# Seven half-size products a pair in the delta-net's projections, and products without a reader behind the norms' sums

## The reference

```python
proj = h @ w_in                      # q, k, v, z for 8 heads of 128, and a, b
qkv = silu(causal_dwconv(qkv, conv_w))          # 4 taps along the sequence
q = l2norm(q) * dk ** -0.5;  k = l2norm(k)
kk = where(strict, (k * beta) @ k.T * decay, 0)
sol = triangular_solve(kk + eye, [v * beta, k * beta * exp(gc)])
... per block: v_new = u - w @ state; o = q exp(g) @ state + qk @ v_new; state = ...
o = o * rsqrt(mean(o * o) + 1e-6) * norm_w * silu(z)
y = o @ w_out
```

```python
y = (x - mean(x)) * rsqrt(var(x) + eps) * g + b
```

## Time and profile before

| | |
|---|---|
| time, median of 3 runs | 2706.67 us (2705.37 to 2707.93) |
| time of the profiled execution | 2705.38 us |
| its span | 2703.6 us, granted clock 0.994 in the mean |
| TensorE busy | 2611.0 us |
| VectorE, ScalarE, GpSimd busy | 1650.5, 682.9, 146.1 us |
| delta-net, heads 0 to 7 | about 86 to 520 us of the span, 55.4 us a head |

### The profile page before, as it was taken

One profiled execution on the slowest core, in us unless ns is written; L12 is line 12 of the kernel. 1 busy time (PEld: TensorE's weight loads), 2 busy tenths in 40 slices (PEclk: granted clock), 3 DMA queues, 4 the chain that ended last, 5 costly groups with the idle time before them and its releaser, 6 DMA issues.

```text
span 2703.6 us, 30522 instructions
## 1 busy us (share of the span) xinstructions
PE 2611.0 (97%) x11992; PEld 1963.3 (73%) x11992; DVE 1650.5 (61%) x2935; ACT 682.9 (25%) x1293; POOL 146.1 (5%) x114
## 2 busy tenths in 40 slices
PE   7999999999999999999999999998999998999999
PEld 2566666568888877888887888885445454888888
DVE  2666667487776454554647877654465486766652
ACT  2334343131111021112102111003443364222200
POOL 0000010010000020000001000001121000000000
PEclk9999999999999999999999999999999999999999
DMA  8121122135443321121122544331021310122121
GB/s 351 63 94 63 63 75 91 54 125 187 159 154 146 117 98 70 67 98 67 63 80 81 190 155 180 143 122 67 31 80 63 125 63 32 63 94 94 60 91 53
DMA packets 25357, 275.02 MB, mean 102 GB/s; under 512 B 3576, under 2 KB 4472, under 8 KB 8192
## 3 DMA queue, kind: packets, MB, share of 16 engines
q1 hardware_dynamic: 21760, 268.39, 26.6%
q10 hardware_dynamic: 3456, 4.69, 0.5%
HBM read 270.97 MB, written 2.10 MB: 101 GB/s over the span
## 4 chain that ended last, share of the span: by engine, by line
PE 90%; DVE 5%; ACT 2%; DMA 1%; issue 1%; POOL 0%; SPq 0%; DVEq 0%; ACTq 0%; POOLq 0%
PE bank L537 29%; PE bank L619 14%; PE bank L2150 10%; PE bank L1264 8%; PE bank L2551 4%; PE bank L412 4%; PE bank L1937 4%; PE bank L1396 2%; PE bank L1414 2%; PE bank L2235 1%; DMA arena<-w_ada 1%; PE bank L2544 1%; PE bank L2999 1%; PE bank L1422 1%; PE bank L2683 1%
## 5 line engine op out<-in xcount | busy, mean ns | idle before, releaser
L537 PE MATMUL bank<-HT,ring 128*128 128x256 f32 x1056 | 252.4, 386 | 9.8 <-ACT HT L945 7.4
L1264 PE MATMUL bank<-HT,ring 128*128 128x512 f32 x512 | 250.3, 597 | 5.6 <-ACT arena L1550 5.6
L537 PE MATMUL bank<-arena,ring 128*128 128x256 f32 x1056 | 249.5, 379 | 0.0
L537 PE MATMUL bank<-arena 128*128 128x256 f32 x1056 | 249.5, 379 | 0.0
L537 PEld LDWEIGHTS bank<-HT,ring 128*128 128x128 f32 x1056 | 202.5, 193 | 45.2 <-issue 15.5
L537 PEld LDWEIGHTS bank<-arena,ring 128*128 128x128 f32 x1056 | 200.6, 190 | 27.3
L537 PEld LDWEIGHTS bank<-arena 128*128 128x128 f32 x1056 | 200.6, 190 | 27.3
L619 PE MATMUL bank<-arena,ring 128*128 128x256 f32 x936 | 207.3, 380 | 9.4 <-ACT arena L691 5.6
L619 PEld LDWEIGHTS bank<-arena,ring 128*128 128x128 f32 x936 | 177.0, 190 | 37.0 <-ACT arena L691 6.8
L1185 ACT ACTIVATE arena<-bank,ffc 128x512 f32<-128x512 f32 x66 | 51.3, 778 | 486.7 <-DVE bank L1093 486.7
L2551 PE MATMUL bank<-HT,ring 128*128 128x512 f32 x320 | 148.2, 604 | 3.0 <-ACT HT L985 3.0
(11 more groups left out here) (470 smaller groups left out, 4216.7 us busy)
## 6 DMA issues: line engine op xcount, KB each, us to landing
ring<-w_ada SPq DMA_DIRECT2D x33, 2048.0 KB, 8.2
ring<-w_up SPq DMA_DIRECT2D x33, 2048.0 KB, 7.6
ring<-w_down SPq DMA_DIRECT2D x24, 1408.0 KB, 6.1
ring<-w_gdn SPq DMA_DIRECT2D x7, 2048.0 KB, 8.7
ring<-w_ret_qk SPq DMA_DIRECT2D x4, 2048.0 KB, 7.7
ring<-w_ret_v SPq DMA_DIRECT2D x4, 2048.0 KB, 7.6
ring<-w_ret_g SPq DMA_DIRECT2D x4, 2048.0 KB, 7.7
ring<-w_ret_out SPq DMA_DIRECT2D x4, 2048.0 KB, 7.6
```

What stands on the lines that cost most here:

```text
L537: last = nc.tensor.matmul(out_, w[:, k, :], x[:, k, :], start=(first and k == 0), stop=(k == 3), skip_group_check=not first)
L1264: last = nc.tensor.matmul(B[u % 2][:, :], w[:, u, k, :], HT[:, k, :], start=(k == 0), stop=(k == KC - 1))
```

## The change

**Projections.** The four units of a head become two pairs, (q, k) and (z, v), and a pair is computed by seven products of half the size where eight would be plain. The weights of a pair are the quarters A11, A12 (first unit, channels 0 to 3 and 4 to 7) and A21, A22; the inputs are cut at channel chunk 4 and at token 256. Four combinations of the inputs (`gdn_T`) are made once on VectorE. Four combinations of the weights are made for each pair on GpSimd, in place in the ring (S3 = A11 - A21, S2 = A22 - S3, S1 = A11 + S2, S4 = A12 - S2). The products M1 to M7 are four steps each of 128 x 128 by 128 x 256, 28 steps a pair, 56 a head. ScalarE keeps M1 and M7 (`m1`, `m7`) and the first result (`c11`); VectorE adds up the others (`t`, `U2`, `c21`, `c22`, `c12`), into SBUF for q, k and v and into the bank for z. The first tap moves to ScalarE (`tap`), the other three stay on VectorE and read the sums from SBUF (`dve_taps`).

**Order.** A head's tail now has 14 steps of the head after next, each level 7 of the next: three ahead of TE, two behind TE and two behind DT. The taps of v move into the head's own levels 1 and 2, vtok from level 2 to 3, gcb from 3 to 4, `normed` from 2 to 5; khat moves behind the inverse of level 6. `zs` is doubled, and the gate is made in the tail before the scan. Table `sel` is no longer loaded; a column of `ident`, broadcast, takes its place (`head_row`).

**Products without a reader.** `pe_keep_clock(n)` multiplies `ident` by itself n times into bank 6, where nothing reads it. It stands behind `pe_sums` of the delta-net's output (13), of the feed-forward networks 0 (13) and 1 (24), of retention (13) and of the mixed output (9), and behind `pe_squares` (11).

```diff
@@ pe_gdn_out, pe_mix_out, pe_down, pe_ret_out and the tensor block @@
             pe_sums(pe, tag, OUT_ORDER[-1], True)
+            pe_keep_clock(pe, 13)
...
+        def pe_keep_clock(pe, n):
+            for _ in range(n):
+                nc.tensor.matmul(B[6][:, 0:P], ident[:, :], ident[:, :], start=True, stop=True)
...
+            if has_mean:
+                pe_keep_clock(pe, 13 if i == 0 else 24)
@@ the projections @@
-                last = nc.tensor.matmul(B[u % 2][:, :], w[:, u, k, :], HT[:, k, :], start=(k == 0), stop=(k == KC - 1))
+        GDN_UNITS = ((0, 1), (3, 2))
+        GDN_ORDER = ("M1", "M7", "M2", "M4", "M5", "M6", "M3")
+        GDN_AHEAD = (0, 2, 4, 6, 8, 10, 12, 13, 14)
+        def pe_steps(pe, h, s0, s1):
+            for s in range(s0, s1):
+                p, name, k = s // PAIR, GDN_ORDER[s % PAIR // 4], s % 4
...
+                elif name == "M7":
+                    out_, w, x, first = Bx[:, 0:TH], A21, gdn_T[2], True
+                    if k == 0:
...
+                        if p:
+                            pe.wait_ge(dve_done, at("dve", "gdn", "c12", h, 0))
+                        elif h:
+                            pe.wait_ge(act_done, at("act", "gdn", "z", h - 1))
+                        pe.wait_ge(pool_done, at("pool", "gdn", "S3", h, p))
...
+                last = nc.tensor.matmul(out_, w[:, k, :], x[:, k, :], start=(first and k == 0), stop=(k == 3), skip_group_check=not first)
@@ the fills @@
+                        s = GDN_AHEAD[-1] + 7 * (l - 1)
+                        pe_steps(pe, h + 1, s + (0, 3, 5, 7)[n0], s + (0, 3, 5, 7)[n1])
@@ ScalarE @@
             def gate(h):
-                act.wait_ge(pe_done, at("pe", "gdn", "proj", h, 3))
-                if h:
-                    act.wait_ge(dve_done, at("dve", "gdn", "gated", h - 1))
-                nc.scalar.activation(G["zs"], B[1][:, :], ACT.Silu).then_inc(act_done, AC.tick("gdn", "z", h))
+                act.wait_ge(dve_done, at("dve", "gdn", "c12", h, 1))
+                if h >= 2:
+                    act.wait_ge(dve_done, at("dve", "gdn", "gated", h - 2))
+                nc.scalar.activation(zs[h % 2], B[1][:, :], ACT.Silu).then_inc(act_done, AC.tick("gdn", "z", h))
@@ VectorE, one head @@
                     if more:
-                        if l < 5:
-                            dve_conv4(dve, h + 1, (l - 1) // 2, 2 * ((l - 1) % 2), 2 * ((l - 1) % 2) + 1)
-                        elif l == 5:
-                            dve_conv4(dve, h + 1, 2, 0, 1)
-                        else:
-                            dve_conv4(dve, h + 1, 2, 3, 4)
-                            khat(h + 1)
+                        if l == 1:
+                            dve_taps(dve, h, 2, 1, 2)
+                        elif l == 2:
+                            ta[1]()
+                            dve_taps(dve, h, 2, 3, 4)
+                        elif l == 3:
+                            ta[4]()
+                        elif l == 4:
+                            dve_taps(dve, h + 1, 1, 3, 4)
+                        elif l == 5:
+                            dve_taps(dve, h + 1, 0, 3, 4)
+                        else:
+                            tb[0]()
                         inverse()
...
+                        if l == 1:
+                            dve_taps(dve, h, 2, 2, 3)
+                            ta[0]()
+                        elif l == 2:
+                            ta[2]()
+                            ta[3]()
+                        elif l == 3:
+                            dve_taps(dve, h + 1, 1, 1, 3)
+                        elif l == 4:
+                            dve_taps(dve, h + 1, 0, 1, 3)
...
+                        elif l == 6:
+                            tb[1]()
+                            tb[2]()
+                            khat(h + 1)
+                            tb[3]()
+                            tb[4]()
                             qhat(h + 1)
@@ GpSimd @@
+            def others(h, p):
+                A11, A12, A21, A22 = gdn_quarters(h, p)
+                pool.wait_ge(pe_done, at("pe", "gdn", "M7", h, p))
+                pool.wait_ge(pool_done, at("pool", "gdn", "S3", h, p))
+                nc.gpsimd.tensor_tensor(A21, A22, A21, ALU.subtract).then_inc(pool_done, PO.tick("gdn", "S2", h, p))
+                pool.wait_ge(pool_done, at("pool", "gdn", "S2", h, p))
+                pool.wait_ge(pe_done, at("pe", "gdn", "M1", h, p))
+                nc.gpsimd.tensor_tensor(A11, A11, A21, ALU.add).then_inc(pool_done, PO.tick("gdn", "S1", h, p))
+                pool.wait_ge(pe_done, at("pe", "gdn", "M2", h, p))
+                nc.gpsimd.tensor_tensor(A12, A12, A21, ALU.subtract).then_inc(pool_done, PO.tick("gdn", "S4", h, p))
...
+            for h in range(GH - 1):
+                third(h + 1, 1)
+                if h + 2 < GH:
+                    third(h + 2, 0)
+                others(h + 1, 1)
+                decay(h + 1)
+                if h + 2 < GH:
+                    others(h + 2, 0)
+                query(h + 1)
```

More of the change, by code:

```diff
@@ new lines, in program @@
+        assert o <= 19968
+        raw_q = region(19968, T)
+        raw_k = wab[:, :, :].rearrange("p k n -> p (k n)")
+        raw_v = sel[:, 0:4, :].rearrange("p i c -> p (i c)")
+        gdn_raw = (raw_q, raw_k, raw_v)
+        zs = [G["zs"], sel[:, 4:8, :].rearrange("p i c -> p (i c)")]
+        gdn_T = [region(21504 + 1024 * n, 4, TH) for n in range(4)]
+        gdn_m1, gdn_m7, gdn_t, gdn_U2 = (HT[:, n, TH:T] for n in range(4))
+        GDN_UNITS = ((0, 1), (3, 2))
+        GDN_ORDER = ("M1", "M7", "M2", "M4", "M5", "M6", "M3")
@@ L1399, in pe_gdn @@
                         osum(h - 1)
-                    if l == 2:
+                    if l == 3:
                         vtok(h)
-                    if l == 3 and more:
+                    if l == 4 and more:
                         gcb(h + 1)
-                    fill(4 * l - 4, 4 * l - 2)
+                    fill(l, 0, 1)
                     pe.wait_ge(dve_done, at("dve", "gdn", "Tm", h, l))
@@ L1569, in act_gdn @@
                 load(name, dst, late_in)
-            for u in range(2):
-                silu(0, u)
-                square(0, u)
+            tap(0, 1)
+            tap(0, 0)
+            keep_m1(0, 1)
+            keep_m7(0, 1)
+            silu(0, 1)
+            square(0, 1)
             raw(0)
-            silu(0, 2)
+            silu(0, 0)
+            square(0, 0)
             gate(0)
             roots(0)
+            keep_m1(1, 0)
             decays(0)
+            tap(0, 2)
+            keep_m7(1, 0)
+            keep_c11(1)
             lower(0)
@@ L1582, in act_gdn @@
                     oroot(h - 1)
+                silu(h, 2)
+                if more:
+                    tap(h + 1, 1)
                 act.wait_ge(pe_done, at("pe", "gdn", "vtok", h))
@@ L1589, in act_gdn @@
                 if more:
-                    silu(h + 1, 0)
-                    square(h + 1, 0)
+                    tap(h + 1, 0)
+                    keep_m1(h + 1, 1)
+                    keep_m7(h + 1, 1)
                     raw(h + 1)
@@ L1601, in act_gdn @@
                 if more:
-                    silu(h + 1, 2)
+                    gate(h + 1)
+                    if h + 2 < GH:
+                        keep_m1(h + 2, 0)
+                    tap(h + 1, 2)
+                    if h + 2 < GH:
+                        keep_m7(h + 2, 0)
+                        keep_c11(h + 2)
                     lower(h + 1)
@@ L1783, in dve_gdn @@
                         inverse()
-                        if l == 2 and h:
+                        if l == 1:
+                            dve_taps(dve, h, 2, 1, 4)
+                        if l == 2:
                             normed(h - 1)
@@ L3251, in _ @@
             pe_squares(pe, "norm4")
+            pe_keep_clock(pe, 11)
             pe_hg(pe)
@@ L3302, in _ @@
                         if u == 0:
-                            table("sel", sel[0:GH], gdn_in)
                             table("ones", ones, gdn_in)
@@ L3461, in layout @@
     A["xT"] = x["x"][0].reshape(T, KC, P).transpose(2, 1, 0)
-    for k in ("ident", "maskL", "maskU", "causal", "ones", "sel", "comb", "headsum", "rot", "cmask", "ret_cos", "ret_sin", "ret_D"):
+    for k in ("ident", "maskL", "maskU", "causal", "ones", "comb", "headsum", "rot", "cmask", "ret_cos", "ret_sin", "ret_D"):
         A[k] = t[k]
```

240 lines of the change are left out of this document (174 added, 66 removed).

## The result

The changed kernel takes 2715.6 us (median of 15 runs, 2707.6 to 2719.8) where the kernel before took 2706.7 in 15 runs beside it: the ratio is 1.0029, 95% interval 1.0021 to 1.0036. The forecast was 2688, 0.7% faster. The profiled execution has a span of 2714.5 us, 10.9 more than before.

The account below looks back on a forecast made before the run. TensorE, busy for 97% of the span, was taken as the bound. Delta-net -12.3 and products without a reader -6.4 bring the span from 2703.6 to 2684.9 us, the median from 2706.67 to 2688.0; range 2668 to 2704.

Parts of the forecast that it names:

- end of the tail: Delta-net tail, before the next head's TE: VectorE's chain up to Tm becomes the limit, TensorE standing 2.2 us for Tm.
- wait for z: Tail of the kernel before: TensorE stands 1.8 us for the gate z, a wait that the change removes.
- S3 of the head after next: GpSimd operation in the delta-net's levels: comes when its load lands, near level 2, against VectorE's PSUM readers.
- Levels, 33.2: Levels 1 to 6 of a delta-net head: 34.8 us falls to 32.7, plus 0.5 of delays beside GpSimd, 33.2.
- Tail, 20.4: From TE's end in level 6 to the next head's first TE: 20.4 us against 20.6, bounded by VectorE.
- Entry, +0.5: Start of the delta-net: fewer product costs, but T sums, S3 and longer queues; +0.5 us, with 2.5 either way.
- Heads 6 and 7, and head 0: Head 6 saves only the levels' 1.6 us; head 7 keeps its products; six heads with a pair ahead save 11.2.
- Delta-net, -12.3: Whole delta-net: six heads -11.2, head 6 -1.6, entry +0.5, together -12.3 us.
- Products, -6.4: Products without a reader keep the clock behind norms 0, 1, 2 and 5: 1.6 us each; nothing behind 3 and 4.
- (e): Rival: eight GpSimd operations hold VectorE's chain for their whole length, 10.2 us a head: 2740, mild form 2715; chance 0.13.
- (b): Rival: GpSimd's work falls in gaps of VectorE, TensorE stays the bound, six heads at -4.5: 2671 us; chance 0.15.

Follow-up runs that it names:

- bridge: The changed kernel with nine more products without a reader ahead of TE of level 1 in heads 1 to 6: 2707.9 us (1.0002).
- narrow: The changed kernel with S1 to S4 on GpSimd cut to 8 of their 512 elements a partition, waits and order kept: 2686.6 us (0.9918).
- reordered kernel: The changed kernel with GpSimd's order changed: S2 and S1 stay in the tail; S4, S3 and qe wait for levels' E subtractions: 2685.2 us (0.9920).
- second run: The changed kernel with the products without a reader left out, so the projections alone: 2720.9 us (1.0042).
- sixth run: The kernel with GpSimd's operations reordered, plus XT's eight multiplications by ALPHA moved from the entry into level 5 of the heads: 2684.5 us (0.9913).

## Why the prediction was wrong

The step that failed is the end of the tail: "So the tail stays at 20.4 against 20.6: VectorE takes the place of z, and TensorE stands 2.2 us for Tm." The wait is there and has its size. It was priced as a wait for a wait, and that was wrong twice. The wait for z was read as 1.8 us, but TensorE was idle for 0.94 us of that, so the idle time rose from 0.94 to 2.12. And behind the longer one TensorE's clock fell in six tails of six. The levels behind stand 3.12 + 3.13 + 1.5 + 1.57 + 3.14 + 1.49 = 14.0 us above the 33.1 of head 0, of which the falls are 9.0, by the bridge. I had worked out what a fall costs behind the norms, from the earlier trace rows, and did not ask the same question of a wait that I was myself lengthening. That these falls need the long wait is shown by the bridge (no wait, no fall) and by the narrow and the reordered S operations (waits of 0.9 us and none, no fall). The weight load that runs beside the first slow stretch (DMA share 0.94) is not their cause either: the reordered kernel has it in the same place (0.97 from 143.2 us on) with the clock at 1.00. That the wait always brings one is not so: head 0 here and head 4 of the second run have it without a fall.

The other 5.0 us belong to a second sentence of the prediction: "S3 of the head after next comes when its load lands, near level 2, against PSUM readers." It meets the ada step of level 2, whose inputs are both in SBUF, and costs a microsecond a head where TensorE is on time: in heads 1 to 5 of the bridge and in head 4 of the second run.

The other terms, against the span of the profiled execution:

- **Levels, 33.2.** Head 0: 33.10, right. Reordered, with the collision of level 2 gone as well: 33.02.
- **Tail, 20.4.** 20.75; the five GpSimd operations of the tail, followed one by one, were right within 0.4 us. This gives 6 x 0.35 = 2 us of the miss.
- **Entry, +0.5 "with two GpSimd lengths (2.5) either way".** It is +5.1, outside its own bounds. VectorE's chain there is longer than I counted: XT's eight multiplications take 5.98 us where they took 2.77, and the last T sum and D and E 1.6 to 2.3 each. The reordered kernel takes back 1.7, with E at its own length. The rest was moved but not removed by the sixth run; what it would take to shorten the entry stays open, ScalarE's queue being next.
- **Heads 6 and 7, and head 0.** I credited head 0 with the saving of the others, though its levels were 34.0 before and not 34.8 (0.7); head 7 and the last tail grew by 0.4 and 0.1.
- **Delta-net, -12.3.** It is +9.6 (the last TE of level 6 starts at 515.3 us instead of 505.7). The difference of 21.9 is 14.0 + 2.1 + 4.6 + 0.7 + 0.5, in the order of the levels of heads 1 to 6, the tails, the entry, head 0, and head 7 with the last tail.
- **Products, -6.4.** Behind norm 0 they give 1.1, norm 2 1.1 to 1.2, norm 5 1.7, and 0.3 behind norms 3 and 4 together; behind norm 1 nothing, since VectorE makes the sums of the next stage late in its turn. That is 4.3 of 6.4. Against it three slow stretches that the kernel before had not, at 1731.9, 1909.4 and 2185.9 us, cost 1.8, 2.5 and 1.4. The middle one stands at a wait for GpSimd that is 1.05 us in the kernel before and 3.58 here: TensorE comes there earlier, by what the products behind norm 3 gave, and waits it away. With the products alone that wait is 3.56 us, with a fall; with the projections alone 1.95, with a fall too. Of the other two, each at a wait as long as in the kernel before, the runs do not show the cause.

Of the rivals, (e) ends on the side where the measurement came out, at 2715 in its mild form. The mechanism that it names is about half of the delta-net's miss: S operations held VectorE's chain for 0.35 us a tail above my count, for a microsecond in level 2 of five heads (hidden here, open in the bridge), and in the entry, but not for their whole length. The clock did the rest, 9.0 of the 21.9 us. Rival (b), TensorE as the bound with 50.9 us a head, is what the reordered kernel shows: 33.02 + 18.48 = 51.5.

## What to carry to other kernels

- When a change puts a wait of some 2 us in front of TensorE, price the wait and the time behind it: here the falls behind six waits of 2.1 us cost another 9 us, where the reordered kernel, without waits or falls in the tails, is worth 22.6 (2707.8 less 2685.2).
- Read a wait from the engine's idle time, not from the chain: the chain's 1.8 us for z held 0.9 us of work.
- Work moved to GpSimd is placed by what VectorE does meanwhile. The same operations in the changed kernel's order cost some 30 us more than in the reordered one: in the two traces 13.6 us in the six tails, 14.4 in the levels of heads 1 to 6 (falls 9.0 by the bridge, the rest mostly the collision in level 2), and 3.4 in the entry and elsewhere. Waits that delay GpSimd were the whole repair.
- Before products are added to keep the clock, look at which waits come next: where falls were taken away others appeared, and the net was 2 to 3.5 us for six places.

## What the hardware did that I had not expected

- The clock fell behind waits of 2.1 us with work on both sides, in six of the changed kernel's seven and six of the seven of the projections alone. The waits of 0.94 for z had not brought it down, and one of 1.26 us at 519.2 in the kernel before had; one of 2.27 us (1020 us) brought it down in one kernel and not in the other. The length of a wait alone does not decide it, and what does is open.
- The falls differ between executions of one kernel. Each trace here is of one; over the changed kernel's 15 runs the mean granted clock goes from 0.989 to 0.995, and the fastest, 2707.6 us, has 0.995.
- A slow stretch hides other losses. Bridged, the clock gave back 7.7 us of 14, since a collision of GpSimd and VectorE that had been covered came to light.
- XT's TENSOR_SCALAR operations, with one SBUF input, also slow down beside GpSimd: in the changed kernel's entry the three that meet its operations take 1.48 to 1.49 us each and the other five 0.41, where all eight took 0.42 in the kernel before with GpSimd idle.
